# Expert weights of a mixture-of-experts encoder step: each matrix loaded in one transfer of 2 MB instead of two of 1 MB

## The reference, cut to what matters

```python
def _moe(h, w_router, b_router, w_gate, w_up, w_down):
    t = h.reshape(B * T, D)
    s = jax.nn.sigmoid((t @ w_router).astype(jnp.float32))
    ...                                   # top group, then top 2 experts: idx, normalised weights w
    gates = jnp.sum(jax.nn.one_hot(idx, N_EXPERTS, dtype=jnp.float32) * w[..., None], axis=1)
    a = jax.nn.silu(jnp.einsum('nd,edf->nef', t, w_gate)) * jnp.einsum('nd,edf->nef', t, w_up)
    a = a * gates[:, :, None].astype(a.dtype)
    return jnp.einsum('nef,efd->nd', a, w_down).reshape(B, T, D)
```

## Time and profile before

| | |
|---|---|
| median of 3 runs | 1699.24 us (1691.51 to 1705.42) |
| profiled execution | 1689.62 us, of which its span is 1687.9 us |
| busy in the span | PE 1431.1 us (85%), DVE 1010.1 (60%), ACT 874.6 (52%), POOL 495.2 (29%) |
| mean granted PE clock | 0.927 |

### The profile page before, as it was taken

How to read it: one execution, slowest core, us unless ns; L and a number is a source line. 1 busy time by engine, 2 the same in 40 slices (tenths; PEclk the granted TensorE clock), 3 DMA queues, 4 the chain that set the end, 5 groups by cost and what they waited for, 6 DMA issues and landing times.

```text
span 1687.9 us, 24152 instructions
## 1 busy us (share of the span) xinstructions
PE 1431.1 (85%) x8611; PEld 1110.8 (66%) x8619; DVE 1010.1 (60%) x1349; ACT 874.6 (52%) x1560; POOL 495.2 (29%) x377
## 2 busy tenths in 40 slices
PE   2499999988937999999936899999788399999991
PEld 0387777755726777887826677777466277887870
DVE  0555542225355988898957444343453668888985
ACT  2233445454125778888733343443431267877872
POOL 1201111110104556666522000000010256666650
PEclk8699999998968999999977999999989599999995
DMA  8355643242054989999961334532422389999974
GB/s 282 111 170 197 205 158 108 71 163 76 0 205 167 354 331 360 368 368 381 364 239 50 102 116 137 169 117 70 163 76 100 115 299 367 371 365 361 372 301 173
DMA packets 148613, 358.70 MB, mean 213 GB/s; under 512 B 18660, under 2 KB 80868, under 8 KB 122420
## 3 DMA queue, kind: packets, MB, share of 16 engines
q1 hardware_dynamic: 136184, 333.25, 54.9%
q0 software_dynamic: 12352, 24.40, 3.9%
HBM read 341.87 MB, written 33.56 MB: 222 GB/s over the span
## 4 chain that ended last, share of the span: by engine, by line
PE 65%; DVE 10%; DMA 8%; issue 6%; ACT 6%; SPq 2%; DVEq 1%; POOLq 0%; ACTq 0%; PEldq 0%; POOL 0%; PEld 0%
PE bank L567 15%; PE bank L569 14%; PE bank L568 14%; DMA ring<-in_w_gate 4%; DVE ring_r L2004 3%; PE bank L323 2%; DMA ring<-in_w_down 2%; PE bank L1496 2%; PE bank L1534 2%; ACT work_r L1997 1%; PE bank L652 1%; PE bank L717 1%; PE bank L1511 1%; PE bank L329 1%; PE bank L959 1%
## 5 line engine op out<-in xcount | busy, mean ns | idle before, releaser
L568 PE MATMUL bank<-ring_r,arena_r 128*128 128x512 f32 x816 | 322.1, 395 | 0.0
L2004 DVE TENSOR_TENSOR ring_r<-ring,work_r 128x1024 fp32r<-128x1024 f32 x102 | 173.5, 1726 | 33.1 <-ACT work_r L1997 33.0
L567 PE MATMUL bank<-ring_r,hT_r 128*128 128x384 f32 x512 | 191.8, 375 | 0.0
L568 PEld LDWEIGHTS bank<-ring_r,arena_r 128*128 128x128 f32 x816 | 156.1, 191 | 30.8
L2004 DVE TENSOR_TENSOR ring_r<-ring,arena_r 128x1024 fp32r<-128x1024 f32 x96 | 157.6, 1676 | 30.6 <-ACT arena_r L1997 30.6
L569 PE MATMUL bank<-ring_r,work_r 128*128 128x384 f32 x512 | 172.8, 337 | 0.0
L568 PE MATMUL bank<-ring_r,hT_r 128*128 128x384 f32 x512 | 172.7, 337 | 0.0
L1997 ACT ACTIVATE hT_r<-ring 128x1024 fp32r<-128x1024 f32 x144 | 144.3, 1054 | 47.0 <-DMA ring<-in_w_gate 43.7
L2004 DVE TENSOR_TENSOR ring_r<-ring,hT_r 128x1024 fp32r<-128x1024 f32 x108 | 144.9, 1369 | 27.0 <-ACT hT_r L1997 25.6
L1997 ACT ACTIVATE arena_r<-ring 128x1024 fp32r<-128x1024 f32 x128 | 127.7, 1052 | 37.9 <-DMA ring<-in_w_down 37.7
L1997 ACT ACTIVATE work_r<-ring 128x1024 fp32r<-128x1024 f32 x136 | 136.6, 1057 | 12.4 <-DMA ring<-in_w_up 12.2
(11 more groups left out here) (358 smaller groups left out, 2923.7 us busy)
## 6 DMA issues: line engine op xcount, KB each, us to landing
ring<-in_w_gate SPq DMA_DIRECT2D x68, 1024.0 KB, 7.4
ring<-in_w_up SPq DMA_DIRECT2D x68, 1024.0 KB, 7.7
ring<-in_w_down SPq DMA_DIRECT2D x68, 1024.0 KB, 8.3
bc<-in_w_ada SPq DMA_DIRECT2D x40, 1024.0 KB, 7.1
bc<-in_w_in_even SPq DMA_DIRECT2D x64, 192.0 KB, 4.2
bc<-in_w_in_odd SPq DMA_DIRECT2D x64, 192.0 KB, 3.7
ring<-in_w_ada SPq DMA_DIRECT2D x4, 2048.0 KB, 11.6
arena<-moe_out SPq DMA_DIRECT2D x8, 1024.0 KB
```

Source lines behind the costliest of these rows:

```text
L567: nc.tensor.matmul(acc, rows_hi, w_hi, start=first, stop=False)
L568: nc.tensor.matmul(acc, rows_hi, w_lo, start=False, stop=False)
L2004: dve.tensor_tensor(r32(piece(m_low[v], q)), piece(m_low[v], q), f32(piece(m_high[v], q)), ALU.subtract).then_inc(MO[f"lo_{c}"], 1)
```

## The change

The load of a slab is one transfer with one semaphore. ACT waits for the whole slab before piece 0, and no more before piece 2. The manual raise of the down semaphore is done once.

```diff
-        MO = sems("mo", "wg0", "wg1", "wu0", "wu1", "wd0", "wd1", "wl0", "wl1", "hi_g", "hi_u", "hi_d", "lo_g", "lo_u", "lo_d",
+        MO = sems("mo", "wg", "wu", "wd", "wl", "hi_g", "hi_u", "hi_d", "lo_g", "lo_u", "lo_d",
...
             for q in pieces:
-                if q in (0, 2):
+                if q == 0:
                     if last_down is not None:
-                        act.wait_ge(MO[f"wl{q // 2}"], 16 * last_down + 16)
+                        act.wait_ge(MO["wl"], 16 * last_down + 16)
                     else:
-                        act.wait_ge(MO[f"w{c}{q // 2}"], 16 * n if c == "d" else 16 * n + 16)
+                        act.wait_ge(MO[f"w{c}"], 16 * n if c == "d" else 16 * n + 16)
...
             def load(c, e, last_down=False):
                 w, k = slabs[c]
                 w = w[bass.ds(e, 1), :, :].rearrange("a (p k) c -> p (a k) c", k=k)
-                for h in range(2):
-                    sp.dma_start(m_low[slab_of(c, last_down)][:, SLAB // 2 * h:SLAB // 2 * (h + 1)].rearrange("p (k c) -> p k c", k=k // 2),
-                                 w[:, k // 2 * h:k // 2 * (h + 1), :]).then_inc(s[f"wl{h}" if last_down else f"w{c}{h}"], 16)
+                sp.dma_start(m_low[slab_of(c, last_down)].rearrange("p (k c) -> p k c", k=k), w
+                             ).then_inc(s["wl" if last_down else f"w{c}"], 16)
...
-            for h in range(2):
-                sp.sem_inc(s[f"wd{h}"], 16)
+            sp.sem_inc(s["wd"], 16)
```

## The result

| | before | after |
|---|---|---|
| median | 1695.4 us (1687.6 to 1705.4, 4 runs) | 1744.1 us (1733.2 to 1746.9, 4 runs) |
| profiled span | 1687.9 us | 1743.4 us |
| ratio, 95% interval | | 1.0279 (1.024 to 1.0319) |

The kernel became slower by 2.8%, 48.7 us between the medians. A second measurement of the same kernel gave 1.0279 again (1.0247 to 1.0311). Direction and range of the prediction hold; the size was forecast too small.

The account below looks back on a forecast made before the run. Expert loops bound it, PE and DMA both almost full, PE's floor 17.8 us a turn. Turns 25.6, last down slabs 3 and clock 3.6 made 32 us on the profiled 1689.6: 1722, range 1700 to 1755.

Parts of the forecast that it names:

- The gate loop: Expert loops: a turn is the larger of PE's own 17.8 us and 11.2 us plus issue to landing.
- The release moves by the second half, and one transfer is no faster: Gate load, empty queue: ACT's piece 0 released 7.7 us after issue, not 5.3; one transfer lands no sooner.
- Rival B: Gate landing: one transfer lands within 6.6 us of issue, making the kernel faster, 1667 us; chance 0.08.
- The term of the turns: 30 expert-loop turns: short ones lifted to 18.9 us, adding 16.6, plus 9 for queue: +25.6 us; upper bound 54.8.
- The clock: PE idle about 1.1 us before each product transpose; two clock falls at 1.8 us each, +3.6 us.
- Rival C: Expert loops: PE loses its clock in many turns, or DVE's down pieces collide with gate's; 1764 us, chance 0.10.
- Up and down cost nothing: Expert loops: whole-slab waits for up and down cost nothing, covered by the later start of PE's turn.
- The last down slabs: End of each layer: nothing hides the later start of ACT's first two pieces; 1.5 us a layer, +3.
- Rival D: Gather of an item's rows lands late behind 16 KB packets; about 12 us, 1734; chance counted within the forecast's 0.58.

Follow-up runs that it names:

- quarters: Kernel before with the gate slab loaded in four transfers of 0.5 MB, a semaphore each; measured 1.0006 of the kernel before.

## Why the prediction was right or wrong

*The gate loop: right.* The turn is the landing plus 11.2 us wherever the clock holds, in the kernel after (19 turns at 11.2 to 11.4), in its repetition (22 at 11.2 to 11.3), and nearly so with two halves and a full wait (11.3 to 11.6). Taking 1.2 us of work out of the rest took 1.2 us from it in 22 of 30 turns.

*The release moves by the second half, and one transfer is no faster: right.* 7.7 us was taken for an empty queue. The first loop load of each layer, which finds the queue empty, landed after 7.9 and 8.1 us, and the least was 7.6. Rival B, which needed less than 6.6 us, falls. So does the 6.8 us that the prediction estimated for 2 MB from the Trainium skill (DMA: Bandwidth & Descriptors, Anatomy of one DMA), whose fit is for transfers issued from GpSimd: the least time of a whole gate load in any profile here, issued from SP, was 7.4 us in one transfer and 7.2 in two.

*The term of the turns: too small, and by two errors of opposite sign.* It was 25.6 us, from a floor of 18.9 and 0.3 us of queue. The queue was 0.74 us in the mean, not 0.3: 8.44 us less 7.7. And the seven long turns of before were left out of the account, although a new floor swallows them as well. The upper bound of this term was also mis-stated: 54.8 us is the sum with the two turns that would have come out negative set to nothing; over all 30, as written, it is 51.5. Landing and the constant rest alone make (11.26 + 8.44 - 18.58) x 30 = 33.5 us.

*The clock: the mis-sized term.* Price nearly right, number wrong. The prediction had two falls at 1.8 us; there were nine at 1.5 us, and the first turn of each layer, where the clock falls as well, lost 3.0 us together. With the small differences of the other turns the longer rests make 16.9 us in the place of 3.6. The wait for the product was foreseen as 1.1 us in every turn. Without the two first turns its mean is (56.2 - 6.3 - 6.5) / 30 = 1.45, and above all it is not even: most waits are 0.6 to 1.2 us, but where a landing comes 1 to 2 us late PE waits 1.6 to 2.8 us, and there the clock mostly goes: of the ten loads that landed after 8.7 us or more, nine have the longer rest. In the repetition it was six of nine. Rival C's first half was therefore at work inside the forecast; its second, DVE's collision with the down pieces, did not show in the kernel after (rest 11.2), but did in the kernel with down alone whole.

*Up and down cost nothing: right for this change, as far as the intervals tell, wrong as a statement.* Behind the gate's wait they are hidden: gate alone whole is as slow as all three (1.0287 and 1.0279). Their cover is that wait, as was said, but what is behind it was given as "up adds up to 1 us a turn" and "down has a whole product's time of slack". It is the reverse: up 5 us in all, down 23 us. The step looked at when PE needs down's pieces, and not at what ACT, in whose queue they stand ahead of gate's pieces, does with the time.

*The last down slabs: right in kind, half in size.* The ends of the layers cost 8.1 us and not 3. In layer 1 the last slab was free to be split at 1691.09 and DVE began the activation's low part at 1697.79, 6.7 us later, where it was 4.7: +2.0, as bounded. The other part comes from the last whole turn of each layer, which stretches like the 30. The start of the stage gave 2.7 us back, which nothing here explains.

*Rival D: wrong.* Packets did become longer. The counts of all packets before and after, the first of them in the earlier trace rows:

```profile
DMA packets 133925, 358.69 MB, mean 206 GB/s; under 512 B 17028, under 2 KB 79236, under 8 KB 120788
```

Packets of 8 KB or more were 26193 and are 13137, half as many for the same bytes. But the gather lands after 7.0 us in the median, not later than the 8.1 of before, and in the kernel after PE's row transposes wait for it in no turn.

*Against which time.* The sum was set against the profiled 1689.6 us, giving 1722. The span grew by 55.5 us, the medians by 48.7: the profiled execution of before lies 6 us below its kernel's median (1689.6 and 1695.4), that of after 1 us above (1745.2 and 1744.1). The sum was 32 us; 48.7 is half as much again. By parts, the 55.5 us of the spans are 33.5 for landing and constant rest (forecast 25.6), 16.9 for the longer rests, nearly all of it behind clock falls (3.6), 8.1 for the ends of the layers (3) and 2.7 given back at the start (nothing). The range held because it was wide enough for this, not because the clock had been sized.

## What to carry to other kernels

When a single buffer is reloaded inside a loop, write the loop as release, issue, landing, fixed rest, and compare it with the busiest engine's floor: one semaphore for the whole gives up the time between first and last bytes, and merging transfers brings nothing when the queue already streams them back to back. Price the waits of PE by their spread and not by their mean, since the waits that were 1 to 2 us longer than usual mostly cost a stretch of half clock too. And a load with plenty of time for its reader can still be on the path of the engine that has to prepare it, if that engine serves it in a fixed order ahead of something urgent.

## What the runs showed of the hardware that was not expected

- PE's clock: a wait of 0.84 us was not followed by a fall; waits of 1.7 us once were and once not the earlier trace rows; that of 2.83 us was, with 0.50 granted from 734 to 737. Counted over the turns without the first of each layer, falls followed nine of the ten waits of 1.6 us or more in the kernel after, six of nine in its repetition, and only two of the ten waits of 1.7 us with quarters. One wait of 2.76 us was followed by none: the turn at 597.62, whose load landed after 9.8 us, has a rest of 11.26.
- A gate load of 2 MB took 7.7 to 8.3 us when down's load had landed before its issue. All 79 that took 8.7 us or more, in six profiles, were issued with down's load still on the way.
- As the first load of a layer's loop, one transfer of 2 MB landed after 7.7 to 8.3 us (six profiles with gate whole, two layers each); two transfers issued together had landed 7.3 to 7.7 us after the first issue (seven profiles). The difference of some 0.5 us did not show in the time.
- DVE's low part of a piece takes 1.21 us alone and 3.43 beside POOL's, which takes 2.46 itself; this sets the long turns of the kernel with quarters. By the Trainium skill (SBUF — State Buffer, SBUF: two separate sides) the two engines share a port pair, which an instruction of DVE with two SBUF inputs or one of GpSimd (POOL) holds to its end while the other waits. The trace agrees: POOL began 0.11 us earlier and ended at 603.14, and DVE ended 1.08 us after that.
